# Up-projection of the MLP: products of a k-tile pair in the order high, high, low, low in place of high, low, high, low

## The reference

```python
def sq_relu_mlp(h, w_in, w_out):
    return jnp.square(jax.nn.relu(h @ w_in)) @ w_out
```

## Time and profile before

| | |
|---|---|
| median of 3 runs | 1516.81 us (1515.51 to 1516.97) |
| profiled execution, its own time | 1515.95 us |
| span in that execution | 1514.1 us |
| mean granted TensorE clock over the span | 0.980 |
| TensorE busy (matmul) | 1431.9 us, 95% |
| VectorE, ScalarE busy | 62%, 46% |

### The profile page before, as it was taken

One profiled execution on the slowest core, in us unless ns is written; L12 is line 12 of the kernel. 1 busy time (PEld: TensorE's weight loads), 2 busy tenths in 40 slices (PEclk: granted clock), 3 DMA queues, 4 the chain that ended last, 5 costly groups with the idle time before them and its releaser, 6 DMA issues.

```text
span 1514.1 us, 22246 instructions
## 1 busy us (share of the span) xinstructions
PE 1431.9 (95%) x9462; PEld 1223.5 (81%) x9462; DVE 938.5 (62%) x1286; ACT 702.6 (46%) x992; POOL 69.0 (5%) x62
## 2 busy tenths in 40 slices
PE   5997988899999989999999999999999999899998
PEld 5777888688888968788889987778888797688887
DVE  6667674566566586665567643656665667575565
ACT  4463232355445546555444345444454535454443
POOL 0014141100001000000000000000000000000000
PEclk9999999899999999999999999999999999999999
DMA  8320000545555531455555554255555544245552
GB/s 302 113 98 2 30 3 2 189 173 195 186 185 206 170 113 53 148 186 194 195 203 207 187 191 151 100 177 170 193 194 189 180 167 139 97 155 194 184 182 80
DMA packets 34660, 230.28 MB, mean 152 GB/s; under 512 B 4048, under 2 KB 4880, under 8 KB 7936
## 3 DMA queue, kind: packets, MB, share of 16 engines
q1 hardware_dynamic: 32752, 223.29, 42.8%
q0 software_dynamic: 1808, 5.56, 1.1%
HBM read 227.77 MB, written 1.05 MB: 151 GB/s over the span
## 4 chain that ended last, share of the span: by engine, by line
PE 83%; DVE 10%; ACT 4%; issue 2%; DMA 0%; SPq 0%; DVEq 0%; POOL 0%; ACTq 0%
PE bank L1598 16%; PE bank L1599 16%; PE bank L1600 16%; PE bank L1673 15%; PE bank L1675 8%; DVE wlo L854 3%; ACT whi L408 2%; PE bank L1879 2%; PE bank L1560 1%; DVE arena L1176 1%; PE bank L1896 1%; ACT arena L566 1%; PE bank L2082 1%; DVE arena L1330 1%; DVE arena L1309 1%
## 5 line engine op out<-in xcount | busy, mean ns | idle before, releaser
L854 DVE TENSOR_TENSOR wlo<-raw,whi 128x2048 fp32r<-128x2048 f32 x208 | 477.0, 2294 | 394.7 <-ACT whi L408 394.4
L408 ACT ACTIVATE whi<-raw 128x2048 fp32r<-128x2048 f32 x208 | 398.7, 1917 | 414.9 <-PE bank L1600 278.4
L1673 PE MATMUL bank<-XHL,whi 128*128 128x512 f32 x1024 | 363.7, 399 | 2.7 <-DVE arena L929 2.1
L1598 PE MATMUL bank<-whi,XHL 128*128 128x512 f32 x896 | 353.5, 395 | 8.9 <-DVE XHL L901 6.8
L1600 PE MATMUL bank<-whi,XHL 128*128 128x512 f32 x896 | 350.5, 391 | 0.0
L1599 PE MATMUL bank<-wlo,XHL 128*128 128x512 f32 x896 | 350.4, 391 | 0.0
L1675 PE MATMUL bank<-XHL,wlo 128*128 128x256 f32 x1024 | 287.7, 281 | 0.0
L1673 PEld LDWEIGHTS bank<-XHL,whi 128*128 128x128 f32 x1024 | 192.7, 188 | 51.1 <-DVE arena L929 3.4
L1598 PEld LDWEIGHTS bank<-whi,XHL 128*128 128x128 f32 x896 | 169.1, 189 | 49.1 <-issue 7.5
L1600 PEld LDWEIGHTS bank<-whi,XHL 128*128 128x128 f32 x896 | 169.0, 189 | 36.4
L1599 PEld LDWEIGHTS bank<-wlo,XHL 128*128 128x128 f32 x896 | 169.3, 189 | 33.8
(11 more groups left out here) (276 smaller groups left out, 1226.1 us busy)
## 6 DMA issues: line engine op xcount, KB each, us to landing
raw<-in_w_mlp SPq DMA_DIRECT2D x128, 1024.0 KB, 4.9
raw<-in_w_rv SPq DMA_DIRECT2D x8, 1024.0 KB, 4.8
raw<-in_w_rg SPq DMA_DIRECT2D x8, 1024.0 KB, 4.8
raw<-in_w_reo SPq DMA_DIRECT2D x8, 1024.0 KB, 4.9
raw<-in_w_k SPq DMA_DIRECT2D x4, 1024.0 KB, 12.7
raw<-in_w_v SPq DMA_DIRECT2D x4, 1024.0 KB, 5.9
raw<-in_w_r SPq DMA_DIRECT2D x4, 1024.0 KB, 4.8
raw<-in_w_rwo SPq DMA_DIRECT2D x4, 1024.0 KB, 4.8
```

What stands on the lines that cost most here:

```text
L408: act.activation(whi[:, u % SPLIT_RING], raw[:, u % RAW_RING], ACT.Copy).then_inc(hi_done, 1)
L854: dve.tensor_tensor(wlo[:, u % SPLIT_RING], raw[:, u % RAW_RING], whi[:, u % SPLIT_RING].bitcast(F32), ALU.subtract).then_inc(lo_done, 1)
L1598: pe.matmul(out_, xh[xs], wh[ws], start=start, stop=False)
L1673: pe.matmul(bank[:, :], whi[ws], XHL[:, kt].rearrange("p h t -> p (h t)"), start=(kt == 0), stop=False)
```

## The change

The inner loop over the four k-tiles of a unit becomes a loop over two pairs of k-tiles. Within a pair, both `whi` products (512 columns) are issued first and then both `wlo` products (256 columns). The call of `feed` (the transposes of the second half of the activations, in the first stretch of the first two MLPs) moves ahead of the loop, at the same point of the program. The number of matmuls, their operands, their weight loads, the waits and the counts are the same.

```diff
-                        for k in range(UK):
-                            kt = kg * UK + k
-                            if t == 0 and kt % 2 == 0:
+                        if t == 2 and kg == 0 and i < 2:
+                            feed(name, 1)
+                        for k2 in range(0, UK, 2):
+                            kt = kg * UK + k2
+                            if t == 0:
                                 pe.wait_ge(turned_lo, SPLIT0[TI[name]] + kt // 2 + 1)
-                            if t == 2 and kt == 0 and i < 2:
-                                feed(name, 1)
-                            ws = (slice(None), u % SPLIT_RING, k, slice(f * P, (f + 1) * P))
-                            pe.matmul(bank[:, :], whi[ws], XHL[:, kt].rearrange("p h t -> p (h t)"),
-                                      start=(kt == 0), stop=False)
-                            ins = pe.matmul(bank[:, 0:T], wlo[ws], XH[:, kt], start=False, stop=(kt == KT - 1))
+                            cols = slice(f * P, (f + 1) * P)
+                            for e in range(2):
+                                pe.matmul(bank[:, :], whi[:, u % SPLIT_RING, k2 + e, cols],
+                                          XHL[:, kt + e].rearrange("p h t -> p (h t)"), start=(kt + e == 0), stop=False)
+                            for e in range(2):
+                                ins = pe.matmul(bank[:, 0:T], wlo[:, u % SPLIT_RING, k2 + e, cols], XH[:, kt + e],
+                                                start=False, stop=(kt + e == KT - 1))
```

## The result

| | before | changed |
|---|---|---|
| median | 1515.51 us (5 runs, 1515.13 to 1516.97) | 1507.70 us (5 runs, 1505.78 to 1508.36) |
| ratio | | 0.9946, 95% interval 0.9935 to 0.9957 |
| profiled execution, own time and span | 1515.95, 1514.1 us | 1507.7, 1505.9 us |

A second comparison, on another occasion and with more runs of before, gave 1508.09 us (5 runs) against 1514.94 us (15 runs), ratio 0.9961 (0.9947 to 0.9975). The medians are 6.9 us apart; the ratio stands for 5.9 us, with an interval from 3.8 to 8.0.

The account below looks back on a forecast made before the run. TensorE's matmul steps, start to start, were taken to bound the up-projection. Groups 2.6, debts 0.7 and first stretches 0.3 us sum to 3.6 us off the 1516.81 us median, giving 1513.2 us; range 1509.3 to 1519.5 us.

Parts of the forecast that it names:

- the 4 us named: Sign to check: TensorE's idle time before the up-projection stays below 4 us.
- the split of the next unit: VectorE's last split before the down-projection still ends about a microsecond ahead of it; slack before was 1.08 us.
- The stake: Up-projection: a group of four matmuls takes 706.7 ns alternating against 693.3 ns at the pure runs' rates.
- C: Rival: nothing changes, the extra belongs to each pair's own instructions; group stays at 706.7 ns, 1516.8 us; chance 22%.
- D: Rival: slower, two short matmuls in a row put TensorE further behind; group 720 ns, 1521.9 us; chance 13%.
- the loss of 13.3 ns a group is put down to its switches, and half of them stay: Up-projection: size switches per group fall from four to two, so a group takes 700 ns.
- The last sentence of the prediction: Mechanism is wrong if groups keep a rhythm set by how the stretch was entered, not by the number of switches.
- a group: Two long and two short up-projection matmuls take 700 ns; over 384 groups in 24 stretches, 2.6 us gained.
- the debt behind a stretch: First 12 down-projection matmuls pay 0.06 us after each of 24 stretches; halved, 0.7 us gained.
- the first stretches: Four first stretches hold 128 groups; a third, 43, counted at 6.67 ns each, 0.3 us gained.
- Rival B: All of the loss goes, groups run at 693.3 ns; gain 7.1 us, so 1509.7 us; chance 23%.
- the clock: Half-speed stretches lie between dense phases; a shift that makes one hit dense work costs or gives back a microsecond.

Follow-up runs that it names:

- e4: Changed kernel with the order by twos only in the first unit of a tile's two, alternation as before in the second; 1512.00 us in a single timing.
- e14: Changed kernel with by twos only in the first tile of the first unit (two groups), alternation behind; 1504.76 us, timed once.
- e3: Changed kernel with four long products in a row, then four short ones, within a unit; 1511.64 us against 1514.74 before, ratio 0.9980.
- e9: Changed kernel with only one group by twos where a stretch begins, alternation behind it; 1513.22 us against 1514.94 before, ratio 0.9986.
- e1: Changed kernel's order in the first two MLPs only, the last two alternating as before; 1511.83 us against 1514.74 before, ratio 0.9982.
- e2: Changed kernel's order in the last two MLPs only, the first two alternating as before; 1510.80 us, ratio 0.9980 to before.
- c1: The changed kernel once more, nothing else altered, with many runs of before beside it; ratio 0.9961 to before.
- e7: Alternating as before, but the low-weight product streams all 512 columns instead of 256; 14.51 us for a stretch of 64 matmuls.

## Why the prediction was wrong

**Right.** TensorE's own steps set the time of this phase. Idle time before the up-projection stayed at 2.2 us, under the 4 us named, and the split of the next unit still ended 1.00 us ahead of `down` (ScalarE's and VectorE's timelines of the changed kernel):

```profile
430.17 1.92 ACT L408 ACTIVATE whi<-raw 128x2048 fp32r<-128x2048 f32 x1 [3.65 <-PE bank L1677]
```
```profile
432.19 2.29 DVE L854 TENSOR_TENSOR wlo<-raw,whi 128x2048 fp32r<-128x2048 f32 x1 [2.87 <-ACT whi L408]
```

432.19 + 2.29 = 434.48, and `down` starts at 435.48 us. The stake was sized rightly: 13.3 ns a group over pure runs, and the debt behind each stretch. That the same list runs in two rhythms was read from the earlier trace rows. Rivals C and D are out: C by e4, e14 and the steps of the changed kernel, D by the groups, at 696.4 ns and not 720. D was nearer in mechanism than in price: the two long ones of a group take 463 and 469 ns in turn, 466 in the mean, just under the 467 ns from which it would have decided, but the two short ones take 231 and not 240.

**The step that failed in mechanism**: "the loss of 13.3 ns a group is put down to its switches, and half of them stay". The loss does not count switches. By fours, with a quarter of the switches, is worse than by twos (e3); alternation with all of them runs at the pure rate behind two groups by twos (e14). In the alternation the loss belongs to a rhythm of three pairs, into which it falls when it comes straight from a run of 512 columns, and behind one group by twos as well (e9). By twos (3.3 ns a group over the pure runs) and by fours (some 7 ns) have losses of their own, which nothing here explains. The last sentence of the prediction had named this as what would make it wrong in its mechanism.

**The terms that were mis-sized by it**:
- a group: 700 forecast, 696.4 measured, so 384 groups gave 24 x 0.153 = 3.7 us, not 2.6;
- the debt behind a stretch: halved in the forecast; measured down from 0.063 to 0.010 us, 24 x 0.053 = 1.3 us, not 0.7;
- the first stretches: 0.3 us forecast. From their start to the next one's, before minus changed, they differ by +0.14, -0.01, -0.26 and +0.35 us, 0.2 us in sum. Half-speed periods sit in the third (changed) and the fourth (both), so this is not told from nothing. The prediction counted only gains here; the parts that already ran fast lost a little, which is why the second gave nothing.

Together 5.2 us against 3.6. Rival B, with 7.1 us, was as near as the forecast: it overstated the group (693.3) and the first stretches.

**The term that was missing**: the clock. The prediction allowed "a microsecond" for it. One wait of 3.5 us alone makes 2.7 us between two executions of nearly the same program, and the part ahead of the first `up` 8.4 us between e1 and e2. Of the first comparison's 7.8 us, 4.9 us are the steps in every trace; c1 with its wider interval agrees with steps alone. For the two profiled executions the remainder is placed: of 8.2 us, 4.9 are steps, 0.2 the first stretches, 2.7 the retention stage, and 0.4 the balance of smaller differences elsewhere. That the remainder of some 2.6 us between the medians had the same cause is argued, not shown, as only profiled runs tell where half-speed periods fell. The range was too narrow at its lower end, since it took B's sum as if nothing but steps could vary: even 1508.09 us of the repetition lies below 1509.3.

## What to carry to other kernels

Take the cost of a matmul stream from start to start, over many, and for every mixture of sizes by itself: no order tried here ran clearly below the sum of the pure rates, and the same list can run 2% above it or on it depending on what ran just ahead. An order that helps for one pair of sizes can hurt for another (512 and 384), so try two or three orders, and try the better one only at the entry of the phase. Look for waits of TensorE of a few microseconds ahead of dense work and try filling them; at the one place tried here 12 idle-time matmuls were worth half as much as the change by the timed runs, a quarter by the traces. Before a difference of a few microseconds is put down to a change, look whether it stands in the part that the change touches: here the untouched first 300 us varied by more than the whole gain.

## What the runs showed of the hardware

- Steady steps at the granted clock of 1.00, with a weight load for each matmul: 226.7 ns for 512 columns (before and e7), 120 ns for 256 (before). Mixed 512 and 384: 406.3 ns a pair.
- 512 and 256 in turn: two stable rhythms, 353.3 ns a pair (repeating every three pairs) and 346.7 (every two pairs or every pair), in stretches of 32 pairs, chosen by one group more or less of another order ahead (e9, e14). In both, a long one takes more than 226.7 ns in the mean (236.7 and 232) and a short one less than 120 (116.7 and 115).
- Behind a mixed stretch the next long matmuls are slower, 0.06 us in all over the first 12 behind the slow rhythm of before and 0.03 behind that of e9, 0.01 behind the fast one, 0.05 by fours and for 384 columns by twos. So part of a phase's cost is paid in the next phase's steps.
- Around the end of 3.5 us without matmuls the clock fell to 1.2 GHz in 13 of 16 traces, around that of 0.8 us in neither of two. The same 16 matmuls took 2.88, 4.17 to 4.56 or 5.49 us.
- In the first 300 us, the same instructions for TensorE in all 18 traces, the time until the first `up` varied from 296.5 to 305.0 us, at a mean granted clock of 0.96 and 0.93 at the two ends.
